# Reordering the entry of the first attention in a two-block transformer forward pass on one core

## The reference

```python
h = x
hn = rms_norm(h, norm_mix_g[0])
proj = hn @ ab_w_in[0]
qa, ka, va, qb, kb, vb = jnp.split(proj, split_ab, axis=-1)
qa = rms_norm(qa.reshape(b, s, A_HEADS, HEAD_DIM), a_q_norm_g[0])
ka = rms_norm(ka.reshape(b, s, A_KV_HEADS, HEAD_DIM), a_k_norm_g[0])
qa = apply_rope(qa, cos_ax, sin_ax)
ka = apply_rope(ka, cos_ax, sin_ax)
o_a = gqa_attention(qa, ka, va)
o_b = dilated_attention(qb, kb, vb, rel_bias)   # reshaped to heads
mix = jnp.concatenate([o_a, o_b], axis=-1) @ ab_w_out[0]
h = h + mix
```

## Time and profile before

| | |
|---|---|
| median of three runs | 1619.18 us (1618.73 to 1619.91) |
| time of the profiled execution | 1617.06 us |
| its span | 1615.0 us |
| PE busy | 1601.1 us, 99% of the span |
| DVE, ACT, POOL busy | 1051.9, 852.6, 43.4 us |

### The profile page before, as it was taken

The page is one execution under the profiler, slowest core; times in us unless marked ns, Lnnn a source line. Parts: engine busy times, 40 slices in busy tenths (PEclk is TensorE's granted clock), DMA queues, the critical chain, the costliest instruction groups (busy, mean ns, idle before and its releaser), DMA issues.

```text
span 1615.0 us, 22343 instructions
## 1 busy us (share of the span) xinstructions
PE 1601.1 (99%) x8597; PEld 1349.6 (84%) x8597; DVE 1051.9 (65%) x1216; ACT 852.6 (53%) x1070; POOL 43.4 (3%) x50
## 2 busy tenths in 40 slices
PE   8999999999999999999999999999999999999999
PEld 6778888978888888888888888888888888888887
DVE  6766565787666676667777666666667554466665
ACT  6565444686444454455785444554445454554443
POOL 1100000000000030000100000000000000000000
PEclk9999999999999999999999999999999999999999
DMA  8635545534544454555445554455545444445550
GB/s 324 231 131 196 208 175 189 175 123 157 209 183 181 182 211 178 198 182 184 155 170 180 202 195 176 182 211 187 193 177 211 158 176 168 175 148 195 204 182 26
DMA packets 43286, 294.26 MB, mean 182 GB/s; under 512 B 4832, under 2 KB 5392, under 8 KB 9296
## 3 DMA queue, kind: packets, MB, share of 16 engines
q1 hardware_dynamic: 39744, 280.84, 47.7%
q0 software_dynamic: 3184, 12.02, 2.3%
q10 hardware_dynamic: 288, 0.39, 0.1%
HBM read 289.18 MB, written 3.15 MB: 181 GB/s over the span
## 4 chain that ended last, share of the span: by engine, by line
PE 96%; DVE 2%; ACT 1%; DMA 1%; issue 0%; POOL 0%; DVEq 0%; POOLq 0%
PE ups L293 26%; PE accs L260 15%; PE accs L262 15%; PE accs L261 15%; PE ups L296 13%; PE accs L293 2%; PE ups L499 1%; PE accs L296 1%; PE ups L1467 1%; PE accs L450 1%; PE accs L447 1%; PE accs L452 1%; DMA tabs<-consts 1%; PE ups L2520 1%; PE ups L1477 1%; PE ups L1086 0%
## 5 line engine op out<-in xcount | busy, mean ns | idle before, releaser
L245 DVE TENSOR_TENSOR wlo<-raw,whi 128x2048 fp32r<-128x2048 f32 x262 | 600.6, 2295 | 212.6 <-ACT whi L241 212.4
L293 PE MATMUL ups<-xhl,whi 128*128 128x512 f32 x1824 | 572.7, 395 | 0.0
L241 ACT CAST whi<-raw 128x2048 fp32r<-128x2048 f32 x264 | 503.6, 1910 | 105.4 <-PE accs L262 105.4
L296 PEld LDWEIGHTS ups<-xhl,wlo 128*128 128x128 f32 x1824 | 342.6, 188 | 80.3
L296 PE MATMUL ups<-xhl,wlo 128*128 128x256 f32 x1824 | 358.3, 278 | 0.0
L293 PEld LDWEIGHTS ups<-xhl,whi 128*128 128x128 f32 x1824 | 282.5, 189 | 5.0
L260 PE MATMUL accs<-whi,hidh 128*128 128x512 f32 x692 | 272.2, 393 | 0.0
L261 PE MATMUL accs<-wlo,hidh 128*128 128x512 f32 x692 | 269.7, 390 | 0.0
L262 PE MATMUL accs<-whi,hidl 128*128 128x512 f32 x692 | 269.4, 389 | 0.0
L262 PEld LDWEIGHTS accs<-whi,hidl 128*128 128x128 f32 x692 | 129.9, 188 | 27.7
L260 PEld LDWEIGHTS accs<-whi,hidh 128*128 128x128 f32 x692 | 129.9, 188 | 24.3 <-issue 0.7
(11 more groups left out here) (268 smaller groups left out, 1394.2 us busy)
## 6 DMA issues: line engine op xcount, KB each, us to landing
raw<-weights SPq DMA_DIRECT2D x264, 1024.0 KB, 4.8
gain<-gains POOLq DMA_DIRECT2D x9, 512.0 KB, 4.0
raw<-weights SPq DMA_DIRECT2D x4, 512.0 KB, 7.2
rel_scratch<-sub_rstd POOLq DMA_DIRECT2D x1, 2048.0 KB, 10.3
big<-rel_scratch POOLq DMA_DIRECT2D x1, 1536.0 KB, 7.6
tabs<-consts POOLq DMA_DIRECT2D x1, 1024.0 KB, 7.6
h<-x_in SPq DMA_DIRECT2D x3, 256.0 KB, 6.9
big<-big POOLq DMA_DIRECT2D x2, 384.0 KB, 4.8
```

The lines of the kernel that those rows point to most:

```text
L241: nc.scalar.copy(whi[:, m % SPLIT, :], raw[:, m % RAW, :]).then_inc(hi_ready, 1)
L245: nc.vector.tensor_tensor(wlo[:, m % SPLIT, :], raw[:, m % RAW, :], whi[:, m % SPLIT, :].bitcast(F32), ALU.subtract).then_inc(lo_ready, 1)
L293: mm = nc.tensor.matmul(bank, W(whi, n, k, j * P, (j + 1) * P), xhl[:, k, :, :].rearrange("p a n -> p (a n)"), start=k == 0, stop=False)
L296: mm = nc.tensor.matmul(bank[:, 0:T], W(wlo, n, k, j * P, (j + 1) * P), xh[:, k, :], start=False, stop=k == KC - 1)
```

## The change

No instruction is added or taken away; all are moves. On PE, three of the nine products of zeros go behind the first transposes, the transposes of quarter 3 go ahead of the products of token block 1, slab 2 is multiplied in one go, and the table product goes behind `turn_kind(0)`. On ACT, the load of `tabs` is issued behind the casts of slab 0; slab 1 is cast ahead of quarter 3, slab 2 ahead of the squares; both of the first two roots come ahead of the cast of slab 3, `root(2)` ahead of `take(0)`, and `vb_copy` ahead of the cast of slab 10. On DVE, slab 1's low parts come ahead of quarter 3's, `normed(1)` ahead of `roped(0)`, and `low(5)` ahead of the loop of heads. POOL's first four loads wait for `x_loaded[3]` alone.

```diff
@@ -398,6 +398,7 @@
                 return mm
 
             turn_part(pe, 0, 0)
+            stay_warm(WARM // 3)
             pe.wait_ge(xh_ready, 1)
             pe.wait_ge(S("half0"), 17)
             part(0, 0, (0, 1), "hh")
@@ -412,10 +413,10 @@
             turn_part(pe, 0, 1)
             pe.wait_ge(lo_ready, 1)
             part(0, 0, (2, 3), "hl")
+            turn_part(pe, 0, 3)
             pe.wait_ge(xh_ready, 2)
             part(0, 1, range(4), "hh")
             part(0, 1, range(4), "hl")
-            turn_part(pe, 0, 3)
             pe.wait_ge(xl_ready, 2)
             part(0, 1, range(4), "lh").then_inc(slab_used, 1)
 
@@ -572,18 +573,18 @@
                 act.wait_ge(mats_loaded, 16)
                 first_high(act, 0, 0)
                 first_high(act, 0, 1)
+                act.dma_start(tabs[:, 0:T], consts[:, C_TAB:C_TAB + T]).then_inc(S("rope_loaded"), 16)
                 act.wait_ge(xh_ready, 1)
-                first_side(act, (2, 1, 3))
+                first_side(act, (2, 1))
                 first_high(act, 1, 0)
                 first_high(act, 1, 1)
-                act.dma_start(tabs[:, 0:T], consts[:, C_TAB:C_TAB + T]).then_inc(S("rope_loaded"), 16)
+                first_side(act, (3,))
+                split_high(act, n + 2)
                 for b in range(2 * TB):
                     act.wait_ge(x_loaded[b], 16)
                 act.sem_inc(h_ready, len(PIECES))
-                square_piece(act, s, 0)
-                split_high(act, n + 2)
-                square_piece(act, s, 1)
-                square_piece(act, s, 2)
+                for p in range(len(PIECES)):
+                    square_piece(act, s, p)
                 return
             else:
                 square_piece(act, s, 0)
@@ -700,10 +701,11 @@
                 first_rest(dve, (0,))
                 first_low(dve, 0, 0)
                 first_low(dve, 0, 1)
-                first_rest(dve, (2, 1, 3))
-                dve.sem_inc(xn_ready, len(PIECES))
+                first_rest(dve, (2, 1))
                 first_low(dve, 1, 0)
                 first_low(dve, 1, 1)
+                first_rest(dve, (3,))
+                dve.sem_inc(xn_ready, len(PIECES))
                 split_low(dve, n + 2)
                 raw_stats(dve, s)
                 return
@@ -1109,14 +1111,13 @@
 
             first_queries(pe).then_inc(slab_used, 1)
             pe.wait_ge(lo_ready, n_ab + 3)
-            project_tokens(n_ab + 2, ab_bank(2), blocks=(0,))
-            table_tensor(pe)
+            project_tokens(n_ab + 2, ab_bank(2)).then_inc(slab_used, 1)
             pe.wait_ge(rstd_ready, ROOTS[0] + 1)
             for t in range(TB):
                 mm = spread(up[2][:, t * P:(t + 1) * P], rstd[:, t:t + 1])
             mm.then_inc(S("row_spread"), 1)
-            project_tokens(n_ab + 2, ab_bank(2), blocks=(1,)).then_inc(slab_used, 1)
             turn_kind(0)
+            table_tensor(pe)
             piece(3, 0)
             turn_kind(1)
             piece(3, 1)
@@ -1227,13 +1228,13 @@
             square(0)
             square(1)
             root(0)
+            root(1)
             high(3)
-            root(1)
             high(4)
             square(2)
             v_copy(2, va, P)
+            root(2)
             take(0)
-            root(2)
             high(5)
             take(1)
             bring_table(ACT.Exp)
@@ -1253,10 +1254,10 @@
                 if c == 7:
                     o_high(6)
                     turned_copy(14)
-                high(5 + c)
                 if c == 5:
                     vb_copy(0)
                     vb_copy(1)
+                high(5 + c)
                 if 2 <= c < 7:
                     o_high(c - 1)
                 if c < 7:
@@ -1359,9 +1360,9 @@
             sums(0)
             sums(1)
             normed(0)
+            normed(1)
             dve.wait_ge(S("rope_ready"), 4)
             roped(0)
-            normed(1)
             low(3)
             sums(2)
             normed(2)
@@ -1373,6 +1374,7 @@
             front(1)
             back(0)
             back(1)
+            low(5)
             for c in range(1, 8):
                 front(2 * c)
                 front(2 * c + 1)
@@ -1385,8 +1387,6 @@
                 if c in (1, 7):
                     o_low(c - 1)
                 back(2 * c + 1)
-                if c == 1:
-                    low(5)
                 low(5 + c)
                 if 2 <= c < 7:
                     o_low(c - 1)
@@ -2722,9 +2722,8 @@
         def _(pool):
             nc.gpsimd.memset(zero[:, :], 0.0).then_inc(filled, 1)
             nc.gpsimd.memset(eps[:, :], EPS).then_inc(filled, 1)
-            pool.wait_ge(S("half1"), 16)
+            pool.wait_ge(x_loaded[3], 16)
             pool.dma_start(rope_rows[:, :], rope_gain.broadcast_to([P, 4 * HD])).then_inc(S("rope_rows"), 16)
-            pool.wait_ge(raw_loaded[1], 16)
             pool.dma_start(rel_sb[:, :].rearrange("p (c h) -> p c h", h=B_HEADS),
                            rel_bias.unsqueeze(1).broadcast_to([NB, COPIES, B_HEADS])).then_inc(S("rel_loaded"), 16)
             pool.dma_start(hot_sb, consts[0:NB, C_HOT:C_HOT + REL]).then_inc(S("rel_loaded"), 16)
@@ -2858,7 +2857,7 @@
         @block.tensor
         def _(pe):
             pe.wait_ge(filled, 1)
-            stay_warm(WARM)
+            stay_warm(WARM - WARM // 3)
             pe.wait_ge(mats_loaded, 16)
             ab_tensor(pe)
             run_feed_tensor(pe, "mlp0", "mlp", 1, 2)
```

## The result

The changed kernel takes 1610.30 us (median of 6 runs, 1610.01 to 1610.57) against 1618.97 us (6 runs, 1617.96 to 1620.06): ratio 0.9946, 95% interval 0.9933 to 0.9958, 8.7 us less. But the two profiled executions, 1617.06 and 1610.57 us, are only 6.5 apart, close to the sum that was made from one of them.

The account below looks back on a forecast made before the run. PE was taken as the bound, busy 1601.1 of 1615.0 us. Gains of 2.8 (entry), 2.85 (`low(5)`) and 0.45 (`vb_copy`) sum to 6.1, so 1619.18 becomes 1613.1 us, range 1611.3 to 1616.0.

Parts of the forecast that it names:

- `vb_copy`: PE's 0.5 us idle before L1102 goes when vb_copy precedes slab 10's cast: 0.45 us gained, bounds 0 and 0.5.
- `low(5)`'s wait: PE's 3.4 us wait for slab 5's low part goes, less 0.55 for the delayed q1 add: 2.85 us gained.
- The entry: From the start to the keys' transposes: slab 2 and roped keys come earlier, 2.8 us gained, between 1.3 and 3.1.
- the moved zeros: Three of nine products of zeros behind PE's first transposes: cost nothing, lying where PE would wait for slab 0's cast.
- the rivals: Four other outcomes: slabs delayed, 15%; low(5) not hidden, 10%; something else holds the later loop, 8%; PE's clock lower, 4%.
- no slab held the entry up by 1.5: First rival, at the entry: small loads delay slab 2 (and 4), 1.5 us of the gain goes, 1614.6; 15%.
- no new wait appeared: Third rival, in the later loop: PE waits for something arriving by its own time, about 1619, no change; 8%.
- The fourth: Rival at PE's start: breaking up the zeros could leave PE at 1.2 GHz, 1627.5 us, slower; 4%.
- I take each gain off both: Whole kernel: gains worked out from one execution, 1617.06 us, are subtracted from it and from the median 2.1 above.
- the terms 3.1, 3.4 and 0.5: Largest gains allowed for the entry, low(5) and vb_copy, giving the lower end of the forecast's own range, 1612.1.

Follow-up runs that it names:

- behind_add: The changed kernel with low(5) moved behind the maxima of heads 2 and 3 and the add for q1: 1610.60 us.
- low5: The kernel before with only low(5) moved ahead of the loop of heads: 1613.23 us, ratio 0.9969.
- pool_back: The changed kernel with POOL's first four loads waiting for the halves of slab 1 again: 1609.88 us.
- warm_back: The changed kernel with all nine products of zeros ahead of the first transposes again: 1609.98 us.
- same_two: The kernel before, unchanged, profiled a third time: 1618.48 us.
- same_three: The kernel before, unchanged, profiled a fourth time: 1618.85 us.
- filled: The kernel before with 13 products of zeros added on PE during its wait for slab 5's low part: 1616.99 us, ratio 0.9992.
- entry: The changed kernel with low(5) and vb_copy put back in their old places, keeping all the entry moves: 1615.77 us, ratio 0.9984.

## Why the prediction was too small

**What held.** `vb_copy`: 0.45 predicted, 0.5 measured by the profiles. `low(5)`'s wait: gone, as in the text, and POOL was held up beside it; that DVE and POOL exclude each other, as in the profile's L927 and in the Trainium skill's "SBUF — State Buffer" (section "Who interferes with whom"), is shown by behind_add, 3.18 against 1.26. Only its price was off, 0.18 for 0.55: in after POOL ended at 45.01 and the add at 45.73, while PE was at `values` until 45.66. In low5 the q1 transposes start at 47.93, which is 48.28 with the 0.35 by which its keys' transposes lie ahead of before's; 48.65 was forecast. With 3.65 in starts for 3.4, the term is 3.5 for 2.85.

The entry: 2.5 at the keys' transposes (34.66 to 32.16) for 2.8. There the step costed "at nothing", the moved zeros, is the one that came out worse: the first products ran 0.43 apart, the 1.2 GHz level, until about 11 us, and slab 2 began at 21.24 for 20.5. In pool_back, which has the same zeros but in whose profile those products are fast, it began at 20.33. The sum of the three by the profiles is 6.5, which is the whole difference of the two profiled executions; by the prediction it is 6.1. None of the rivals came true in its size: no slab held the entry up by 1.5 and no new wait appeared. The fourth, PE's clock behind the broken-up zeros, came true in small: 6 products at the lower level where some 30 were needed to lose the gain, worth 0.3 by the medians and 0.6 by the profiles of after and warm_back.

**What failed** is the sentence "I take each gain off both". The terms were made from one execution, 1617.06, and taken off a median that lay 2.1 above it, as if those 2.1 were the same on both sides. They were not. The execution read was the one profile in four without the dip, and by the clocks of the runs 5 of 59 are like it: in the others the 3.4 us wait for slab 5's low part is followed by about 3.4 us of PE at 1.2 GHz. From the start of the piece to the next transposes this costs 1.49, 1.26 and 1.17 in the three profiles (4.47, 4.24 and 4.15 less 2.98); where the fall came later, some of it lies behind those transposes: to the end it is another 0.3 in same_two and 0.4 in same_three, so the dip costs 1.5 to 1.6 each time. `filled` takes it away without making the low part come earlier, 1.5. The wait was mis-sized by what it does to the work behind it: its term in the median is 3.5 + 1.5 = 5.0, which is low5's ratio. With the entry's 2.5 and `vb_copy`'s 0.5 that makes 8.0 of the 8.7 measured. (A slip of 0.1 besides: 1619.18 less the terms 3.1, 3.4 and 0.5 is 1612.2, not 1612.1, which changes nothing here.)

The prediction had a clock rival, but pointed it the wrong way: it asked whether the change could lower the clock at the zeros, not whether the idle time that it removes was lowering the clock already. The row that should have raised the question is the first of the earlier trace rows, the only wait above 3 us; the 2.1 between the profiled execution and the median, and runs 1.2 apart, were the second sign. The Trainium skill has the rule, in "TensorE: Matmul & The Clock Gate" (Part 1, "HAM oscillation — how this bites in real kernels"): a long enough idle gap between bursts of products brings the lower clock back, and the next burst starts at it. The runs agree in part: 3.3 to 3.6 us of idle were followed by the lower clock in three profiles of four of before, and not in that of entry; and here the next burst started at 2.4 GHz, 0.12 apart, and fell 0.7 to 1.4 us later.

**What stays open.** Some 0.7 of the 8.7 has no term of its own. Part of it is that after's profiled execution, 1610.57, was the slowest of its six, 0.3 above their median; the rest would fit the runs of before at a mean clock of 0.998, which take 2.2 more than 1617.06 where the profiled dips cost 1.5 to 1.6, but no profile shows where those runs lose it. Before's own medians also differ by 0.5 between groups. That splitting the zeros delays the clock's rise is likely from the profiles (four of five against none of nine), not settled, and its price of 0.3 to 0.6 is at the edge of what the runs tell. What decides in which execution the clock falls was not tried.

## What to carry to other kernels

When the profiled execution lies off the median by more than the runs scatter elsewhere, take another profile before making the sum: the terms belong to the execution read, and a loss that comes in only some executions is invisible in the one that escaped it. The mean granted clock of each run, set beside its time, shows such a loss without any further profile. Price a long wait of PE by the wait and by the work behind it at half clock; a wait near 3.4 us was worth 5.0 here. Where such a wait cannot be removed, filling it with idle products recovered 1.5, with no change to what is computed.

## What the hardware showed unexpectedly

The granted clock fell not during the idle time but after PE had resumed work: by the means of the 2 us stretches 0.7, 1.3 and 1.4 us after, in the three profiles, and it was low for about 3.4 us each time. So a piece of work can begin at the full rate and lose it in its middle. The scatter of the whole kernel, 3.9 us in the 22 runs of one group, went with this idle time: 0.6 to 1.4 in every kernel without the idle gap, 2.1 to 3.9 in every set of runs with it.
